# One layer of a hybrid decoder on one core: the second mixer's gate made in the first chunk, its group norm reordered, and the first output weights split by halves

## The reference, cut to what matters

```python
g = jax.nn.sigmoid(gl7) @ rwkv_g2
mu = jnp.mean(y, axis=-1, keepdims=True)
var = jnp.mean(jnp.square(y - mu), axis=-1, keepdims=True)
y = (y - mu) * lax.rsqrt(var + RWKV_GN_EPS) * gn_w + gn_b
bonus = jnp.sum(r * k7 * rwkv_r_k, axis=-1, keepdims=True) * v7
o_rwkv = (y + bonus).reshape(B, T, RWKV_WIDTH) * g
out = jnp.concatenate([o_gla, o_rwkv], axis=-1) @ w_out
```

## Time and profile before

| | us |
|---|---|
| median of 3 runs | 1875.35 |
| lowest and highest run | 1875.28, 1878.07 |
| the profiled execution | 1873.54 |
| its span, first to last instruction | 1871.8 |

### The profile page before, as it was taken

The page is one execution under the profiler, slowest core; times in us unless marked ns, Lnnn a source line. Parts: engine busy times, 40 slices in busy tenths (PEclk is TensorE's granted clock), DMA queues, the critical chain, the costliest instruction groups (busy, mean ns, idle before and its releaser), DMA issues.

```text
span 1871.8 us, 32911 instructions
## 1 busy us (share of the span) xinstructions
PE 1751.0 (94%) x14031; PEld 1106.9 (59%) x14031; DVE 665.4 (36%) x1444; ACT 470.1 (25%) x778; POOL 211.8 (11%) x295
## 2 busy tenths in 40 slices
PE   5689999999989999899899999999999999999997
PEld 2268779988856666799644444445444454444544
DVE  1145554464673544643322222222221222222224
ACT  3044333344531211344411111111111111111114
POOL 1000000011028880343000000000000000000000
PEclk9889999999999999899999999999999999999998
DMA  9989885585388779341799999999999999999993
GB/s 365 419 285 336 295 326 144 188 263 158 131 313 332 302 307 376 100 162 46 320 420 430 428 429 427 430 427 430 427 430 427 430 427 430 427 430 427 430 427 155
DMA packets 124944, 629.64 MB, mean 336 GB/s; under 512 B 10469, under 2 KB 78493, under 8 KB 83360
## 3 DMA queue, kind: packets, MB, share of 16 engines
q1 hardware_dynamic: 118974, 608.45, 80.9%
q0 software_dynamic: 5120, 17.44, 2.7%
q10 hardware_dynamic: 754, 2.33, 0.3%
HBM read 618.65 MB, written 9.56 MB: 336 GB/s over the span
## 4 chain that ended last, share of the span: by engine, by line
PE 42%; DMA 13%; DVE 1%; issue 1%; SPq 0%; ACT 0%; POOL 0%; DVEq 0%; POOLq 0%; ACTq 0%
PE pb L2681 24%; DMA ring<-in_w_exp_gate 13%; PE pb L2655 4%; PE pb L2661 2%; PE pb L2689 2%; PE pb L2032 2%; PE pb L2033 2%; PE pb L2034 1%; PE pb L2662 1%; PE pb L2570 0%; DVE xt L1830 0%; SPq L502 0%; PE pb L2731 0%; PE pb L2577 0%; PE pb L2728 0%
## 5 line engine op out<-in xcount | busy, mean ns | idle before, releaser
L2681 PE MATMUL pb<-ring,pj 128*64 128x512 f32 x2048 | 460.0, 602 | 23.9 <-DMA ring<-in_w_exp_gate 23.0
L2681 PEld LDWEIGHTS pb<-ring,pj 128*64 128x64 f32 x2048 | 149.2, 138 | 298.8 <-issue 294.7
L2032 PE MATMUL pb<-ht_parts,ring_parts 128*128 128x264 f32 x1056 | 309.5, 293 | 7.3 <-DVE ring_parts L1304 6.2
L2033 PE MATMUL pb<-ring_parts 128*128 128x264 f32 x1056 | 302.1, 286 | 0.0
L2034 PE MATMUL pb<-ring_parts 128*128 128x264 f32 x1056 | 301.8, 286 | 0.0
L2689 PE MATMUL pb<-ring,pj 128*64 128x512 f32 x1024 | 223.3, 594 | 0.0
L2032 PEld LDWEIGHTS pb<-ht_parts,ring_parts 128*128 128x128 f32 x1056 | 202.0, 191 | 24.3 <-issue 16.0
L2033 PEld LDWEIGHTS pb<-ring_parts 128*128 128x128 f32 x1056 | 202.0, 191 | 0.0
L2034 PEld LDWEIGHTS pb<-ring_parts 128*128 128x128 f32 x1056 | 200.9, 190 | 0.0
L1304 DVE TENSOR_TENSOR ring_parts<-ring,ring_parts 128x2048 fp32r<-128x2048 f32 x50 | 114.6, 2292 | 173.9 <-ACT ring_parts L789 173.8
L2689 PEld LDWEIGHTS pb<-ring,pj 128*64 128x64 f32 x1024 | 72.2, 137 | 138.9 <-issue 136.9
(11 more groups left out here) (474 smaller groups left out, 1959.2 us busy)
## 6 DMA issues: line engine op xcount, KB each, us to landing
ring<-in_w_exp_gate SPq DMA_DIRECT2D x64, 2048.0 KB, 15.2
ring<-in_w_exp_up SPq DMA_DIRECT2D x64, 2048.0 KB, 17.2
ring<-in_w_exp_down SPq DMA_DIRECT2D x64, 2048.0 KB, 15.7
ring<-in_w_ada SPq DMA_DIRECT2D x32, 2048.0 KB, 14.8
ring<-in_w_in SPq DMA_DIRECT2D x24, 2048.0 KB, 9.4
pj<-in_w_ada SPq DMA_DIRECT2D x32, 1024.0 KB, 7.8
ring<-in_w_ada_final SPq DMA_DIRECT2D x16, 2048.0 KB, 13.0
ring<-in_w_out SPq DMA_DIRECT2D x8, 2048.0 KB, 8.6
```

The source lines that it names most:

```text
L2032: pe.matmul(out, hi[:, k, :], ht_lo[:, k, :], start=(k == 0), stop=False)
L2033: pe.matmul(out, lo[:, k, :], ht_hi[:, k, :], start=False, stop=False)
L2681: last = pe.matmul(pb[step // 2][SLOT * q:SLOT * q + SLOT, :], xg[:, k, SLOT * q:SLOT * q + SLOT], w[q][:, j, :], start=(k == 0), stop=(k ...
```

## The change

- The gate of all 256 prompt tokens is made in chunk 0, in four pieces of two tiles, and that of the samples in a fifth; ScalarE copies each from PSUM bank 5 to SBUF (`gates` in the free `xt`, `gates_s` in `g2`). The gates in chunks 1 to 3 and in the tail go. The scratch of the turned shifts moves to a free part of the ring.
- The formula becomes `y * gn_w * g * root + (bonus + gn_b) * g`. `bonus_gated` and `gn_scale` are four operations of all 512 (or 64) columns on VectorE that need no variance; `gn_finish` keeps a reciprocal, a product and a sum. In the tail they are placed ahead of the variance of chunk 3.
- The samples' turn, sum, centring, squares and variance move into chunk 3. In the tail the samples' finish stands ahead of chunk 3's.
- In the tail, TensorE takes chunk 3's sum ahead of the turn of the state; ScalarE takes the first weight half, the samples' root, the state copy, and then chunk 3's squares; the copies of x (`x_out`) go behind `out_hi`.
- The weight halves of output tiles 0 and 1 are made in two pieces of eight k-blocks each, on ScalarE and on GpSimd; TensorE needs only the first to begin.
- Order numbers of the group norm's semaphores come from lists; several semaphores of the expert stage and of the samples' moves are shared.

The core of the diff (`w_hi_out` gives the count that a weight piece has on its semaphore; `gn_ps`, `gn_act` and `gn_dve` give a step's semaphore and count; the shared semaphores are left out):

```diff
-            def out_weight_lo(t):
-                pool.wait_ge(S("w_hi"), IN_TILES + t + 1)
-                s, m = out_slot(t // 2), t % 2
-                pool.tensor_tensor(weight_tile(ring_r, s, m), weight_tile(ring, s, m), w_hi[:, m].bitcast(F32),
+            def out_weight_lo(t, part):
+                pool.wait_ge(S("w_hi"), w_hi_out(t, part))
+                s, m, ks = out_slot(t // 2), t % 2, slice(8 * part, 8 * part + 8)
+                pool.tensor_tensor(weight_tile(ring_r, s, m)[:, ks], weight_tile(ring, s, m)[:, ks], w_hi[:, m, ks].bitcast(F32),
...
-            out_weight_lo(0)
-            out_weight_lo(1)
+            for part in range(2):
+                for t in range(2):
+                    out_weight_lo(t, part)
...
+            def gates_out(i):
+
+                act.wait_ge(S("gate_ps"), i + 1)
+                act.copy(gates[:, 2 * i:2 * i + 2, :], pb[5][:].rearrange("p (t n) -> p t n", n=NP_)).then_inc(S("gate_ev"), 1)
...
                     gn_square(c - 1)
+                else:
+                    gates_out(0)
+                    gates_out(1)
...
+                if c == 0:
+                    gates_out(2)
...
+                else:
+                    gates_out(3)
...
+                if c == 0:
+                    act.wait_ge(S("gate_ps"), 5)
+                    act.copy(gates_s, pb[5][:, 0:8 * NS].rearrange("p (t n) -> p t n", n=NS)).then_inc(S("gate_ev"), 1)
+                if c == NCH - 1:
+                    gn_square(SAMPLES)
...
             act.wait_ge(S("ck_y"), 2 * NCH)
-            out_weight_hi(0)
-            gn_square(NCH - 1)
-            out_weight_hi(1)
-            gn_sqrt(NCH - 1)
-            gn_square(NCH)
-            gn_sqrt(NCH)
+            low, high = slice(0, 8), slice(8, KD)
+            out_weight_hi(0, low)
+            gn_sqrt(SAMPLES)
+            act.wait_ge(*once("sr_ps"))
+            act.copy(sr_new, eight(0)).then_inc(once("sr_evac")[0], 1)
+            gn_square(LAST)
+            out_weight_hi(1, low)
+            gn_sqrt(LAST)
+            out_weight_hi(0, high)
+            out_weight_hi(1, high)
+            for i in range(2):
+                act.wait_ge(*gn_dve(LAST, "finish"))
+                act.wait_ge(S("state_out"), 48)
+                out_hi(slice(8 + 4 * i, 12 + 4 * i))
             x_out(0)
             x_out(1)
-            for i in range(2):
-                act.wait_ge(S("gn_dve"), gn_step(NCH, 2))
-                act.wait_ge(S("state_out"), 48)
-                out_hi(slice(8 + 4 * i, 12 + 4 * i))
...
+            def gate_of(n):
+                return gates[:, :, GROUPS[n]] if n < NCH else gates_s
+
+            def wide8(at, n):
                 g = GROUPS[n]
-                dve.wait_ge(S("gn_ps"), gn_step(n, 0))
-                dve.scalar_tensor_tensor(out=y8[:, :, g], in0=sums(bank, g), scalar=-1.0 / RD, in1=y8[:, :, g],
+                return vec(at, 8, g.stop - g.start)
+
+            def bonus_gated(n):
+                g = GROUPS[n]
+                dve.wait_ge(S("gate_ev"), 5)
+                link(dve.tensor_tensor(bonus[:, :, g], bonus[:, :, g], wide8(V_GBI, n), ALU.add))
+                dve.tensor_tensor(bonus[:, :, g], bonus[:, :, g], gate_of(n), ALU.mult).then_inc(S("bonus_dve"), 1)
...
-            def gn_variance(n, bank):
+            def gn_scale(n):
                 g = GROUPS[n]
-                dve.wait_ge(S("gn_ps"), gn_step(n, 1))
...
-            def gn_finish(n, bank):
+                dve.wait_ge(*gn_act(n, "square"))
+                link(dve.tensor_tensor(y8[:, :, g], y8[:, :, g], wide8(V_GW, n), ALU.mult))
+                link(dve.tensor_tensor(y8[:, :, g], y8[:, :, g], gate_of(n), ALU.mult))
+
+            def gn_variance(n, bank, at=0):
...
-                dve.wait_ge(S("gn_act"), 2 * n + 2)
+                dve.wait_ge(*gn_ps(n, "squares"))
+                dve.tensor_scalar(rb[:, :, g], sums(bank, g, at), 1.0 / RD, GN_EPS, ALU.mult, ALU.add).then_inc(S("gn_dve"), 1)
+
+            def gn_finish(n):
+                g = GROUPS[n]
+                dve.wait_ge(*gn_act(n, "root"))
                 link(dve.reciprocal(rb[:, :, g], rb[:, :, g]))
-                for t in range(8):
-                    last = dve.scalar_tensor_tensor(out=y8[:, t, g], in0=y8[:, t, g], scalar=vecs[:, V_GW + t:V_GW + t + 1],
-                                                    in1=rb[:, t, g], op0=ALU.mult, op1=ALU.mult)
-                link(last)
-                for t in range(8):
-                    last = dve.scalar_tensor_tensor(out=y8[:, t, g], in0=y8[:, t, g], scalar=vecs[:, V_GBI + t:V_GBI + t + 1],
-                                                    in1=bonus[:, t, g], op0=ALU.add, op1=ALU.add)
-                link(last)
-                dve.wait_ge(S("gn_ps"), gn_step(n, 2))
-                dve.tensor_tensor(y8[:, :, g], y8[:, :, g], sums(bank, g), ALU.mult).then_inc(S("gn_dve"), 1)
+                link(dve.tensor_tensor(y8[:, :, g], y8[:, :, g], rb[:, :, g], ALU.mult))
+                dve.wait_ge(S("bonus_dve"), n + 1)
+                dve.tensor_tensor(y8[:, :, g], y8[:, :, g], bonus[:, :, g], ALU.add).then_inc(S("gn_dve"), 1)
...
                     if l == 4 and c > 0:
                         gn_centre(c - 1, 6)
+                        if c == NCH - 1:
+                            dve.wait_ge(*once("ys_ps"))
+                            for h in range(2):
+                                last = dve.tensor_copy(y8[RD * h:RD * h + RD, :, NP_:NT],
+                                                       pb[5][0:RD, 0:P].rearrange("p (b t h) -> p h t b", b=NS, h=2)[:, h])
+                            last.then_inc(once("y_all")[0], 1)
+                            dve.wait_ge(*once("y_all"))
                     if l == 5 and c > 0:
                         gn_variance(c - 1, 6)
+                        if c == NCH - 1:
+                            gn_centre(SAMPLES, 5, P)
...
-                    gn_finish(c - 1, 6)
+                    bonus_gated(c - 1)
+                    gn_scale(c - 1)
+                    gn_finish(c - 1)
+                if c == NCH - 1:
+                    gn_variance(SAMPLES, 5, P + 8 * NS)
...
-            gn_centre(SAMPLES, 2)
+            gn_centre(LAST, 6)
             dve.memset(misc[:, 520:532], 1.0)
             dve.memset(acc_s, 0.0)
-            gn_variance(L, 3)
-            gn_variance(SAMPLES, 2)
-            gn_finish(L, 6)
-            gn_finish(SAMPLES, 2)
+            bonus_gated(LAST)
+            gn_scale(LAST)
+            gn_variance(LAST, 3)
+            bonus_gated(SAMPLES)
+            gn_scale(SAMPLES)
+            gn_finish(SAMPLES)
+            gn_finish(LAST)
...
+            def gate(i):
+
+                if i == 0:
+                    pe.wait_ge(S("late_in"), 16)
+                    pe.wait_ge(S("ck_ve"), 3)
+                else:
+                    pe.wait_ge(S("gate_ev"), i)
+                n, ts, g = (NP_, range(2 * i, 2 * i + 2), slice(0, NP_)) if i < 4 else (NS, range(8), GROUPS[SAMPLES])
+                for t in ts:
+                    at = (t - ts[0]) * n
+                    last = pe.matmul(pb[5][:, at:at + n], g2[:, t * P:(t + 1) * P], pj[:, TG7, g], start=True, stop=True)
+                last.then_inc(S("gate_ps"), 1)
...
                     whole(6, y8, GROUPS[c - 1]).then_inc(S("gn_ps"), 1)
+                else:
+                    gate(0)
+                if c == NCH - 1:
+                    pe.wait_ge(S("ck_ve"), c * 3 + 3)
+                    pe.wait_ge(S("ys_row"), RD // SI)
+                    pe.transpose(pb[5][0:RD, 0:P], y_row, ident[:]).then_inc(once("ys_ps")[0], 1)
                 inverse_grow(3)
+                if c == 0:
+                    gate(1)
                 ada_piece(c + 4, 7)
...
-                    pe.wait_ge(S("gn_act"), 2 * c - 1)
+                    pe.wait_ge(*gn_act(c - 1, "square"))
                     whole(6, ra, GROUPS[c - 1]).then_inc(S("gn_ps"), 1)
+                else:
+                    gate(2)
+                if c == NCH - 1:
+                    pe.wait_ge(*once("y_all"))
+                    whole(5, y8, GROUPS[SAMPLES], P).then_inc(S("gn_ps"), 1)
                 inverse_grow(4)
+                if c == 0:
+                    gate(3)
...
                 if c > 0:
-                    pe.wait_ge(S("gn_dve"), gn_step(c - 1, 1))
+                    pe.wait_ge(*gn_dve(c - 1, "variance"))
+                else:
+                    gate(4)
...
-                if c > 0:
-                    pe.wait_ge(S("late_in"), 16)
-                    pe.wait_ge(S("ada_mod"), c + 5)
-                    gate(c - 1, 6)
+                if c == NCH - 1:
+                    pe.wait_ge(*gn_act(SAMPLES, "square"))
+                    whole(5, ra, GROUPS[SAMPLES], P + 8 * NS).then_inc(S("gn_ps"), 1)
...
                     ada_piece(c + 5, 3)
+            pe.wait_ge(S("ck_yev"), NCH)
+            pe.wait_ge(S("ada_mod"), 8)
```

(17 more changed lines are left out.)

111 lines of the change are left out of this document (54 added, 57 removed).

## The result

| | us |
|---|---|
| before, median of 20 runs | 1877.1 (1870.3 to 1880.7) |
| changed, median of 20 runs | 1881.0 (1872.9 to 1886.2) |
| ratio | 1.0025, 95% interval 1.0014 to 1.0037 |
| changed, profiled execution | 1885.6, span 1883.8, clock 0.966 |
| changed, second series and profile (e12) | 1880.3, ratio 1.0036 (1.0018 to 1.0055), span 1874.4 |

The change costs 0.25% by the ratio, 4.7 us (3.9 us between the two medians), which is the sum that was forecast (+4.7). The terms of that sum are another matter.

The account below looks back on a forecast made before the run. Expert stage bound by DMA bytes, so earlier delays reach the end one for one. Terms 5.6 + 0 - 3.3 + 0.2 + 2.2 = +4.7 us on the median 1875.35 gave 1880.0; range 1869.5 to 1886.

Parts of the forecast that it names:

- Gates made once: In chunk 0, the added gate matmuls on TensorE would be hidden by nothing and cost 5.6 us.
- The zero for the gates removed from chunks 1 and 2: In chunks 1 and 2, dropping 2.0 us of gates each only lengthens the adaLN wait from 0.69 to 2.7; saving 0.
- The shift in chunks 1 and 2: Chunk 0's 5.6 us delay makes VectorE's masks in chunks 1 and 2 meet GpSimd less: -3.3 us in all.
- The tail: After chunk 3, the shorter finish is spent waiting for GpSimd's weight pieces: +0.2 us, chunk 3's 0.7 included.
- strict turns: In the tail, VectorE and GpSimd alternate, so four small samples' products each wait for a GpSimd instruction, until 775.9.
- The clock: A TensorE pause of 6 to 8 us before the output tiles' second halves starts them at half rate: +2.2 us.

Follow-up runs that it names:

- e12: The changed kernel unaltered, measured and profiled a second time; 1.0036 of the kernel before.
- e3: The changed kernel with GpSimd's first weight-low piece held until VectorE has finished the samples' normalization; 1.0015 of the kernel before.
- e7: The changed kernel with the last chunk's product on the gate reading the gate from PSUM, made there by eight more matmuls; 1.0038 of the kernel before.
- e9: The changed kernel with each of GpSimd's four weight-low pieces waiting for the result of the one before; 1.0041 of the kernel before.
- e2: The changed kernel with each of chunk 0's five gate pieces cut to one matmul of 8 columns; 1.0010 of the kernel before.
- e4: The kernel before with the gates of chunks 1 and 2 cut from eight matmuls to one each; 1.0001 of the kernel before.
- e8: Reworked changed kernel: gates back in each chunk, samples finished first, last chunk's operations from the gate on with one PSUM input, weight halves rearranged; 0.9975 of before.
- e11: e8 with the last chunk's and the samples' gates made later, behind the state's turn and the sum of squares; 0.9983 of the kernel before.
- e1: The changed kernel with every gate matmul of chunk 0 issued twice; 1.0064 of the kernel before.
- e5: The kernel before with GpSimd's products and sums of the samples' recurrence cut to one element per partition; 0.9973 of the kernel before.
- e10: The changed kernel with the five gate pieces moved behind the last adaLN piece of chunk 0; 1.0111 of the kernel before.
- e6: The changed kernel with GpSimd's products and sums of the samples' recurrence cut to one element per partition; 1.0000 of the kernel before.

## Why the prediction was right in the sum

The sum was right and the account behind it was not: two of its five terms missed in opposite directions. Stages of chunks, in us, means over profiles of kernels with the same code there; gates in chunk 0: the changed kernel, e3, e7, e9, e12; without: before, e2, e4, e8, e11 (chunk 3: before, e2, e4).

| | without | with | difference | predicted |
|---|---|---|---|---|
| start of chunk 0 | 542.2 | 540.1 | -2.1 | 0 |
| chunk 0 | 58.5 | 64.3 | +5.8 | +5.6 |
| chunks 1 and 2 | 113.1 | 115.6 | +2.6 | -3.3 |
| chunk 3 to the state's turn | 48.3 | 47.7 | -0.6 | |
| state's turn to second halves | 23.5 | 21.1 | -2.4 | +0.2 (with chunk 3) |
| second halves to the end of tile 0 | 3.3 | 5.5 | +2.2 | +2.2 |

(The last two rows are of before and of the changed kernel alone; the second series has 21.1 and 4.8. For chunks 1 and 2 the five profiles with the gates run from 112.6 to 117.8, those without from 111.7 to 114.0, so the +2.6 is good to 2 or 3 us: enough to exclude -3.3, not to tell it from none. e1, with two sets of gates, is not in the means.)

**Gates made once: right.** +5.8 in the means, 5.5 for one more set in e1, 5 in the ratios of e1 and e2. The 7.6 of the first profile has 10.7 us of half rate in chunk 0, where before had 6.8. The zero for the gates removed from chunks 1 and 2 is right too: e4 gained nothing, and the wait for the weights grew to 2.0 to 3.0 us in every full kernel without those gates (2.7 predicted).

**The shift in chunks 1 and 2: this step failed.** Its mechanism is there: the waits for VectorE in the two chunks fell from 6.4 us (mean of the five kernels without the gates in chunk 0) to 2.7, 3.7 less, where 2.7 were forecast, and e5 shows that GpSimd makes them. But TensorE's stops without a releaser grew by about as much, from 1.2 to 4.7 us; in e3, e7, e9 and e12 one of 2.1 to 2.6 stands ahead of the second adaLN piece of chunk 1:

```profile
620.76 3.38 PE L2005 MATMUL pb<-ring,ct 128*32 128x512 f32 x16 [2.35 <-issue]
```

(this is e12), and four of the five kernels have three stretches of half rate in these chunks where before has two. Instead of -3.3 the chunks gave +2.6, against which chunk 0 started 2.1 earlier in the mean; at the state's turn the kernels with the gates stand at 767.7, those without at 761.7. The earlier start lies ahead of all changed code on TensorE and may be chance.

What the stops wait for is neither the weight stream (e10) nor GpSimd's recurrence (e6 has them too, 4.1 and 1.6). They are no lost records either: chunks 1 and 2 have 1034 matmul records each in all five, counted by their starts. The traces point to TensorE's own instructions. The DMA view lists, beside data, packets of a kind `instruction`; in e12 between 560 and 625 us, on queue q8, it has nine of 16 KB each:

```profile
q8 instruction: 9, 0.15, 0.9%
```

The last of these ran from 618.35 to 619.25, and the stop from 618.41 to 620.76. In all fourteen traces each of the 84 stops of over 0.25 us without a releaser between 540 and 800 us ends 1.2 to 1.6 us after the end of such a packet, while TensorE's waits of over 0.9 us with a releaser end anywhere from 0 to 24 us after one. This is read from times and no run varied it; why a packet comes late in one kernel and not in the next is open. In e1 the stops of chunks 1 and 2 are 0.5 us, the waits for VectorE 2.1, and the two chunks take 107.2, 5.8 less than the mean without gates: where the stops stay away, the shift pays (in a profile 8 us faster than e1's median). In e2, whose masks wait as before (6.4), the stops are 0 and the chunks take 114.0.

**The tail: right that it meets GpSimd, wrong where and how long.** The prediction assumed strict turns, from the group between 607 and 611, and let the samples' small products pay. Those rows were of chained instructions, each waiting for the result of the last. The weight pieces are not chained, and the first product with two SBUF inputs waited through two (5.97 to 6.00 in all six profiles with this tail), in e7 through four (8.87). With chained pieces (e9) the predicted picture came out in the main, three of the small products at 1.7 to 2.4 us. The Trainium skill, "SBUF — State Buffer", "SBUF: two separate sides", says that the one of the two that starts first gets the ports for its whole instruction and that the other fully blocks. The trace agrees with the block, since each long product ends just behind a piece, but not with the order: the product's record starts 0.74 us before that of the first piece, it needs 0.69, and it still came behind two pieces. The block cost 5.3 us and still the tail from the state's turn to the second halves is 2.4 shorter than before, and chunk 3 is 0.6 shorter: -3.0 where +0.2 was forecast, a term mis-sized by 3.2.

**The clock: right.** The pause ahead of the second halves is 6.03 us (0.80 before), the records behind it are 0.22 apart and half rate lasts from 789.7 to 796.5. From there to the first use of tile 0 it takes 5.48 us against 3.27. The others bear it out: in e7, e8, e9, e11 and e12 pauses of 4.2 to 9.5 us are followed by 4.8 to 5.7 us, in e3 a pause of 1.62 by 3.26. e4, which has the tail of before, weakens it: a pause of 1.96 and then 4.80, so the order of before has given both times (e5 again 3.27), and the +2.2 rests on which of them is taken as its own.

So the shift's -3.3 was wrong by 5.9 us to one side, the tail's +0.2 by 3.2 to the other, and the earlier start of chunk 0 takes 2.1 more; 5.5 us is what the rows of the table add up to, 4.7 what the ratio says. The forecast stood on two errors that cancelled: that the sum agrees is luck to that extent.

## What to carry to other kernels

Move work off a path only to where an engine really waits: the gates cost nothing in chunks 1 and 2, ahead of a wait for DMA, and 5.8 us in chunk 0, which has no such wait. Before putting a VectorE product of two SBUF inputs beside GpSimd, look whether GpSimd's instructions are chained: unchained ones can keep a product of 0.2 us out until the last has ended. An operand in PSUM, even the reciprocal's output, takes VectorE out of it (e8). Where an engine stops without a releaser, look in the DMA view for instruction packets. And a margin won from one wait is only a margin if no other stop grows in its place, so read the same stage in several profiles before pricing a shift.
